# The seams between mixer and FFN of a four-layer decoder trunk: norm wholly on VectorE, another order of blocks, products and tile halves

## Chip, cores and metric

The kernel runs on 1 core of one Trainium2 chip. The metric is the device time of one execution in microseconds, shown as the median of several runs.

## What is computed

Two layers, each a token mixer and a gated convolutional FFN, with a normalised residual after each: `x <- LayerNorm(ALPHA * x + sublayer(x)) * g + b`. The input has 512 tokens of width 1024, all in float32. The reference, cut to its frame:

```
def layer_norm(x, g, b):
    mu = jnp.mean(xf, -1, keepdims=True)
    var = jnp.mean(jnp.square(xf - mu), -1, keepdims=True)
    return ((xf - mu) * lax.rsqrt(var + LN_EPS)).astype(x.dtype) * g + b

def conv_ffn(x, w_up, conv_w, conv_b, w_down):
    h = causal_dwconv(x @ w_up, conv_w) + conv_b
    a, b = jnp.split(h, 2, axis=-1)
    return (jax.nn.silu(a) * b) @ w_down

for i in range(DEPTH):                      # DEPTH = 2
    m = gated_deltanet(...) if i % 2 == 0 else diff_attention(...)   # both end in @ w_out
    x = layer_norm(DEEPNORM_ALPHA * x + m, ln_mix_g[i], ln_mix_b[i])
    f = conv_ffn(x, ffn_w_up[i], ffn_conv_w[i], ffn_conv_b[i], ffn_w_down[i])
    x = layer_norm(DEEPNORM_ALPHA * x + f, ln_ffn_g[i], ln_ffn_b[i])
```

## The kernel before

Tokens lie in four blocks (tb 0 to 3) of 128, one per partition, in `x_tok`. A product in float32 is made of three: each operand is split in a high part (`*_hi`, a copy by ScalarE) and the rest (`*_lo`, a subtraction by VectorE), and TensorE multiplies hi*hi, hi*lo and lo*hi into one PSUM bank. Weights come in chunks of 512 KB: SyncE loads a chunk into one of two `raw` slots as soon as the split of the chunk that had the slot two chunks before is done (`load`, which waits for `lo_ready`); ScalarE writes `w_hi`, VectorE `w_lo`. Every engine has its own list of instructions, written out by hand in the order in which it runs them, and engines meet only at semaphores.

The change is about the two seams, one a layer (l = 0 after the gated DeltaNet, l = 1 after the attention), where the mixer's output is normed and handed to the FFN:

- *Last products of the mixer.* A `mixer_unit(l, tb, k)` adds head k's part (chunk k of `w_out`) to block tb: two halves of 512 columns, three products each. During the last head's step TensorE fills its gaps with such units of blocks 0 and 1 (heads 0 to 6; attention: heads 0 to 5). What is left follows: block 2's heads, the last heads of blocks 0 to 2 (these wait for the last head's `u_hi` and `u_lo`), then `mixer_rest`: all heads of block 3. When block 3 has used one of the last eight chunks, its slot is free for the FFN's weights (`chunk_done`).
- *Norm.* `stats(i, tb)` on VectorE adds the residual from PSUM (L1184), takes statistics (L1188, L1190). `deviation` on ScalarE takes the square root. `scaled(i, tb)` on VectorE: for blocks below `POOL_TB` = 2, (x - mean) * rstd in one step of 1024 columns (L1204), after which GpSimd multiplies by gamma (L564) and adds beta (L566), 128 x 1024 each; for the others VectorE does (x - mean) * gamma (L1199) and two halves of x * rstd + beta (L1208). Norms are numbered i = 0 to 3; 0 and 2 are the mixers', 1 and 3 the FFNs'. `load_gb(i)` loads gamma and beta into one buffer once the norm before is through.
- *Turn and split.* `turn_out(i, tb)` on TensorE waits for the block's norm and transposes it in eight steps (L1415) into two banks. `hi(j, tb)` on ScalarE (L600) and `lo(j, tb)` on VectorE (L938) make `x_hi` and `x_lo` of it.
- *The first four tiles of up-products.* `up_tile(l, r, cols)` is tile r for a half of the tokens: 24 products (three for each of 8 chunks of the width) of 256 columns. The early half needs the splits of blocks 0 and 1, the late half those of 2 and 3, and each tile needs its weight chunk split (`split_up` on ScalarE, L784, and `split` on VectorE, L328). `ffn_start` orders them: early halves of tiles 0 and 1, turn of block 2, early halves of 2 and 3, turn of block 3, the four late halves. Then a loop runs over the other 40 tiles.

VectorE's list for a seam is `mixer_out(l)` (L1214) and ScalarE's the function of the same name (L763). VectorE norms blocks 0, 1 and 2, splits weight chunks 0 and 1, block 0, weight chunks 2 and 3, blocks 1 and 2, and then norms and splits block 3. The turns of blocks 0 and 1 stand in `mixer_rest`, ahead of block 3's last head and behind it.

## Time and profile before

| | |
|---|---|
| median of 3 runs | 1574.72 us (1572.68 to 1575.71) |
| profiled execution | 1572.31 us; span 1570.5 us |
| mean granted TensorE clock | 0.977 |
| TensorE busy | 1469.8 us (94%) |
| VectorE busy | 869.2 us (55%) |
| ScalarE busy | 626.1 us (40%) |
| GpSimd busy | 130.3 us (8%) |
| TensorE's share of the chain that ended last | 76% |

The span runs from the first to the last instruction; the execution's own time is 1.8 us longer. Products overlap, so the start of one to the start of the next is the pace, and it is shorter than the time of one. An idle time in brackets stands ahead of the instruction in its row, with what released it. Seam 0 lies at about 480 to 540 us of the span, seam 1 at about 1146 to 1208.

### The profile page before, as it was taken

Reading aid. Unit: us, or ns where it says so; the run is one execution under the profiler, and the core shown is the slowest. Engines: PE = TensorE matmul, PEld = TensorE weight load, DVE = VectorE, ACT = ScalarE, POOL = GpSimd, SP = SyncE. Lnnn points to the kernel's source line nnn. Section 1 sums busy time; section 2 is a strip of 40 time slices with the busy share of each in tenths; the row PEclk is TensorE's granted clock in tenths of the full one; section 3 lists DMA queues with packets and bytes.
Section 4 is the critical chain, followed back from the end, with each engine's and each line's share of the span. In section 5 each row is a group of like instructions: output and inputs, shape, how many; then the busy total and the mean of one; then the engine's idle time right before and its main releaser. Section 6 shows DMA issues by size and latency. Waiting matters only on the chain.

```text
span 1570.5 us, 20997 instructions
## 1 busy us (share of the span) xinstructions
PE 1469.8 (94%) x7474; PEld 1204.3 (77%) x7474; DVE 869.2 (55%) x1288; ACT 626.1 (40%) x997; POOL 130.3 (8%) x121
## 2 busy tenths in 40 slices
PE   6899999999889699999999999999996999999997
PEld 5688778887777678888788777677676788887886
DVE  5556655666455466666522544777755666665225
ACT  4743554345422244444411224565522444444220
POOL 4101110111012000000000201111020000000002
PEclk8999999999999899999999999999998999999999
DMA  5211111111120133333322131112211333333321
GB/s 165 57 52 48 47 46 40 47 47 47 41 68 14 54 95 95 104 93 93 134 101 101 44 104 54 41 54 80 83 38 54 97 96 101 93 93 134 107 95 67
DMA packets 157726, 118.85 MB, mean 76 GB/s; under 512 B 5898, under 2 KB 145644, under 8 KB 157676
## 3 DMA queue, kind: packets, MB, share of 16 engines
q1 hardware_dynamic: 157676, 118.17, 24.6%
q8 instruction: 33, 0.54, 0.1%
q14 instruction: 17, 0.14, 0.0%
HBM read 116.04 MB, written 2.11 MB: 75 GB/s over the span
## 4 chain that ended last, share of the span: by engine, by line
PE 76%; DVE 10%; ACT 5%; issue 4%; POOL 2%; DMA 2%; SPq 1%; ACTq 0%; DVEq 0%; POOLq 0%
PE bank L1449 13%; PE bank L1451 13%; PE bank L1450 13%; PE bank L1437 7%; PE bank L1439 7%; PE bank L1438 7%; PE bank L1512 5%; PE bank L1505 3%; DVE w_lo L328 1%; PE bank L1787 1%; PE bank L1805 1%; DVE x_tok L1184 1%; PE bank L1746 1%; DVE bn L1188 1%; DVE x_tok L1199 1%
## 5 line engine op out<-in xcount | busy, mean ns | idle before, releaser
L1449 PE MATMUL bank<-x_hi,w_hi 128*128 128x512 f32 (+1 forms) x1160 | 463.3, 399 | 29.3 <-DVE x_lo L938 25.8
L1451 PE MATMUL bank<-x_hi,w_lo 128*128 128x512 f32 (+1 forms) x1160 | 442.3, 381 | 0.0
L1450 PE MATMUL bank<-x_lo,w_hi 128*128 128x512 f32 (+1 forms) x1160 | 441.7, 381 | 0.0
L328 DVE TENSOR_TENSOR w_lo<-raw,w_hi 128x1024 fp32r<-128x1024 f32 x196 | 246.6, 1261 | 311.6 <-ACT w_hi L323 298.9
L1449 PEld LDWEIGHTS bank<-x_hi,w_hi 128*128 128x128 f32 x1160 | 223.4, 193 | 68.4 <-DVE w_lo L328 24.2
L323 ACT ACTIVATE w_hi<-raw 128x1024 fp32r<-128x1024 f32 x188 | 196.9, 1050 | 191.9 <-PE bank L1439 154.3
L1451 PEld LDWEIGHTS bank<-x_hi,w_lo 128*128 128x128 f32 x1160 | 222.4, 192 | 41.5
L1450 PEld LDWEIGHTS bank<-x_lo,w_hi 128*128 128x128 f32 x1160 | 223.5, 193 | 37.3 <-issue 3.4
L1437 PE MATMUL bank<-w_hi,u_hi 128*128 128x512 f32 x416 | 165.9, 399 | 14.3 <-issue 5.7
L1439 PE MATMUL bank<-w_hi,u_lo 128*128 128x512 f32 x416 | 163.7, 393 | 0.0
L1438 PE MATMUL bank<-w_lo,u_hi 128*128 128x512 f32 x416 | 163.5, 393 | 0.0
L1437 PEld LDWEIGHTS bank<-w_hi,u_hi 128*128 128x128 f32 x416 | 79.1, 190 | 33.6 <-issue 11.3
L1439 PEld LDWEIGHTS bank<-w_hi,u_lo 128*128 128x128 f32 x416 | 79.0, 190 | 16.8
L1438 PEld LDWEIGHTS bank<-w_lo,u_hi 128*128 128x128 f32 x416 | 79.1, 190 | 16.5 <-issue 0.5
L564 POOL TENSOR_TENSOR x_tok<-x_tok,gb 128x1024 f32<-128x1024 f32 x8 | 19.3, 2408 | 854.3 <-DVE x_tok L1204 854.3
L823 ACT ACTIVATE u_hi<-acc_b 128x512 f32 (+1 forms) x44 | 27.8, 632 | 116.0 <-DVE acc_b L1277 116.0
L650 ACT ACTIVATE scr<-bank,vec 128x512 f32<-128x512 f32 x24 | 16.4, 684 | 116.7 <-PE bank L1451 116.7
L1033 DVE SCALAR_TENSOR_TENSOR scr<-bank,vec,scr 128x511 f32<-128x511 f32 (+2 forms) x72 | 53.6, 745 | 9.3 <-ACT scr L650 5.4
L820 ACT ACTIVATE acc_a<-acc_a 128x512 f32<-128x512 f32 x44 | 27.8, 632 | 77.6 <-DVE acc_a L1272 77.6
L1269 DVE SCALAR_TENSOR_TENSOR acc_b<-bank,vec,acc_b 128x511 f32<-128x511 f32 x44 | 33.0, 749 | 39.0 <-ACT acc_b L816 39.0
L816 ACT ACTIVATE acc_b<-bank,vec 128x512 f32<-128x512 f32 x44 | 34.2, 777 | 49.7 <-PE bank L1451 49.7
L1280 DVE TENSOR_TENSOR u_lo<-acc_b,u_hi 128x512 f32 (+1 forms) x44 | 30.5, 692 | 39.9 <-ACT u_hi L823 39.9
(268 smaller groups left out, 1925.6 us busy)
## 6 DMA issues: line engine op xcount, KB each, us to landing
raw<-in_ffn_w_up SPq DMA_DIRECT2D x88, 512.0 KB, 3.7
raw<-in_ffn_w_down SPq DMA_DIRECT2D x44, 512.0 KB, 3.2
raw<-in_gdn_w_in SPq DMA_DIRECT2D x32, 512.0 KB, 4.1
raw<-in_diff_w_in SPq DMA_DIRECT2D x24, 512.0 KB, 3.7
raw<-in_gdn_w_out SPq DMA_DIRECT2D x8, 512.0 KB, 3.3
raw<-in_diff_w_out SPq DMA_DIRECT2D x8, 512.0 KB, 3.3
x_tok<-in_x SPq DMA_DIRECT2D x4, 512.0 KB, 5.7
ROW<-decay_rows SPq DMA_DIRECT2D x8, 256.0 KB, 4.6
```

Source lines behind the costliest of these rows:

```text
L323: nc.scalar.activation(w_hi[:, s, :], raw[:, (base + r) % RAW, :], ACT.Copy).then_inc(hi_ready, 1)
L328: nc.vector.tensor_tensor(w_lo[:, s, :], raw[:, (base + r) % RAW, :], w_hi[:, s, :].bitcast(F32), ALU.subtract).then_inc(lo_ready, 1)
L816: nc.scalar.activation(acc, b[:, :], ACT.Identity, bias=fcb(l, t), scale=fcw(l, 2, t)).then_inc(f_act, 1)
L1033: ins = nc.vector.scalar_tensor_tensor(acc[:, sh:T], bank[r % 2][:, 0:T - sh], gcw(3 - sh, i * 8 + h), acc[:, sh:T], ALU.mult, ALU.add)
L1437: nc.tensor.matmul(out, hi[:, k, tok], high[:, cols], start=(k == 0), stop=False)
L1438: nc.tensor.matmul(out, hi[:, k, tok], low[:, cols], start=False, stop=False)
L1439: ins = nc.tensor.matmul(out, lo[:, k, tok], high[:, cols], start=False, stop=(k == K - 1))
L1449: nc.tensor.matmul(out, hi, x_hi[:, k, cols], start=(k == 0), stop=False)
L1450: nc.tensor.matmul(out, hi, x_lo[:, k, cols], start=False, stop=False)
L1451: ins = nc.tensor.matmul(out, lo, x_hi[:, k, cols], start=False, stop=last)
L1505: ins = nc.tensor.matmul(out, lhsT(n), rhs(n), start=True, stop=True)
L1512: ins = nc.tensor.matmul(halves(X(e, i)[:, c], s, h), lhsT[e][:, n, :], halves(rhs[e][:, n, :], s, h), start=True, stop=True)
```

## The change

- `POOL_TB` becomes a list, `[0, 2, 0, 2]`: in the mixers' norms (0 and 2) all four blocks take VectorE's form, and GpSimd has no part; in the FFNs' norms nothing changes.
- VectorE's `mixer_out`: stats of blocks 0 and 1, affine part of both, weight split 0, split of block 0, weight split 1, split of block 1, then stats 2, weight split 2, stats 3, weight split 3, affine parts 2 and 3, splits of blocks 2 and 3. ScalarE's list follows that order.
- Last products: 4 heads of block 2 first (HELD = 4, where there were 7 and 6), then the last heads of blocks 0 and 1 alone, then the other 4 heads of block 2, then block 3, with the turn of block 0 ahead of its head 3 and that of block 1 ahead of its head 5. In the attention, two of block 2's heads stand ahead of the turn of the last head's output (`turned_out`).
- `ffn_start`: all four early halves in a row, then the turns of blocks 2 and 3, then the late halves.
- The numbers on which engines wait are made anew for the new order (`norm_steps`), and `load_gb` waits for GpSimd only where it had a part before.

```diff
--- before.py
+++ after.py
@@ -68,7 +68,7 @@
              [(0, 1), (2, 3), (4, 5), (6, 7)]]
 TURN_BANKS = [OUT_BANKS[1], OUT_BANKS[0], OUT_BANKS[1], OUT_BANKS[2]]
 UP_BANKS = [(0, 1, 2, 3), (0, 1, 4, 5)]
-POOL_TB = 2
+POOL_TB = [0, 2, 0, 2]
 
 
 C_GDN_IN = 0
@@ -415,8 +415,9 @@
             def load_gb(i):
                 names = ("ln_mix_g", "ln_mix_b") if i % 2 == 0 else ("ln_ffn_g", "ln_ffn_b")
                 if i > 0:
-                    sp.wait_ge(ln_dve, LN_N * i)
-                    sp.wait_ge(ln_pool, LP_N * i)
+                    sp.wait_ge(ln_dve, LN_START[i])
+                    if LP_START[i] > 0:
+                        sp.wait_ge(ln_pool, LP_START[i])
                 for j in range(2):
                     sp.dma_start(gb[:, j, :], a[names[j]][i // 2].partition_broadcast(P)).then_inc(gb_loaded, 16)
 
@@ -461,16 +462,16 @@
             load_down(1)
             for tb in range(NT):
                 rows_out = a["out"][0, tb * P:(tb + 1) * P, :]
-                if tb < POOL_TB:
-                    sp.wait_ge(ln_pool, LP_N * 3 + LP["b", tb])
+                if tb < POOL_TB[3]:
+                    sp.wait_ge(ln_pool, LP[3, "b", tb])
                     sp.dma_start(rows_out, x_tok[:, tb, :]).then_inc(stored, 16)
                 elif tb < NT - 1:
-                    sp.wait_ge(ln_dve, LN_N * 3 + LN["y", tb, 1])
+                    sp.wait_ge(ln_dve, LN[3, "y", tb, 1])
                     sp.dma_start(rows_out, x_tok[:, tb, :]).then_inc(stored, 16)
                 else:
                     for half in range(2):
                         c = slice(half * T, (half + 1) * T)
-                        sp.wait_ge(ln_dve, LN_N * 3 + LN["y", tb, half])
+                        sp.wait_ge(ln_dve, LN[3, "y", tb, half])
                         sp.dma_start(rows_out[:, c], x_tok[:, tb, c]).then_inc(stored, 16)
             sp.wait_ge(stored, 16 * (NT + 1))
 
@@ -556,16 +557,15 @@
                                             ALU.add).then_inc(d_pool, 1)
 
             def affine(i):
-                for tb in range(POOL_TB):
+                for tb in range(POOL_TB[i]):
                     y = x_tok[:, tb, :]
                     if tb == 0:
                         pool.wait_ge(gb_loaded, 32 * (i + 1))
-                    pool.wait_ge(ln_dve, LN_N * i + LN["n", tb])
+                    pool.wait_ge(ln_dve, LN[i, "n", tb])
                     nc.gpsimd.tensor_tensor(y, y, gb[:, 0, :], ALU.mult).then_inc(ln_pool, 1)
-                    pool.wait_ge(ln_pool, LP_N * i + LP["g", tb])
+                    pool.wait_ge(ln_pool, LP[i, "g", tb])
                     nc.gpsimd.tensor_tensor(y, y, gb[:, 1, :], ALU.add).then_inc(ln_pool, 1)
 
-            affine(0)
             affine(1)
             pool.wait_ge(v_out, 2 * NT)
 
@@ -588,7 +588,6 @@
                     rope_cos(h + 1, kind)
                 pool.wait_ge(t_pe, 1 + TP_N * h + TP["pv"])
                 take_v(h + 1)
-            affine(2)
             affine(3)
 
 
@@ -751,7 +750,7 @@
             step(HEADS - 1, 1, False)
 
             def deviation(i, tb):
-                act.wait_ge(ln_dve, LN_N * i + LN["mv", tb])
+                act.wait_ge(ln_dve, LN[i, "mv", tb])
                 nc.scalar.activation(std[:, tb:tb + 1], mv[:, tb, 1:2], ACT.Sqrt, bias=bias_ln).then_inc(ln_act, 1)
 
             def load_sqrt():
@@ -765,15 +764,15 @@
                 i, j = 2 * l, 2 * l + 1
                 deviation(i, 0)
                 deviation(i, 1)
-                deviation(i, 2)
                 split_up(l, 0)
                 split_up(l, 1)
                 hi(j, 0)
+                hi(j, 1)
                 split_up(l, 2)
+                deviation(i, 2)
                 split_up(l, 3)
-                hi(j, 1)
+                deviation(i, 3)
                 hi(j, 2)
-                deviation(i, 3)
                 hi(j, 3)
 
             def split_up(l, r):
@@ -1175,7 +1174,7 @@
             def stats(i, tb):
 
                 def own(*key):
-                    dve.wait_ge(ln_dve, LN_N * i + LN[key if len(key) > 1 else key[0]])
+                    dve.wait_ge(ln_dve, LN[i, *key])
 
                 for half in range(2):
                     wait_done(dve, ST_OUT[i], tb, half)
@@ -1193,14 +1192,14 @@
             def scaled(i, tb):
 
                 y, mean, rstd = x_tok[:, tb, :], mv[:, tb, 0:1], std[:, tb:tb + 1]
-                if tb >= POOL_TB:
-                    if tb == POOL_TB:
+                if tb >= POOL_TB[i]:
+                    if tb == POOL_TB[i]:
                         dve.wait_ge(gb_loaded, 32 * (i + 1))
                     nc.vector.scalar_tensor_tensor(y, y, mean, gb[:, 0, :], ALU.subtract, ALU.mult).then_inc(ln_dve, 1)
                 dve.wait_ge(ln_act, NT * i + tb + 1)
                 nc.vector.reciprocal(rstd, rstd).then_inc(ln_dve, 1)
-                dve.wait_ge(ln_dve, LN_N * i + LN["inv", tb])
-                if tb < POOL_TB:
+                dve.wait_ge(ln_dve, LN[i, "inv", tb])
+                if tb < POOL_TB[i]:
                     nc.vector.tensor_scalar(y, y, mean, rstd, ALU.subtract, ALU.mult).then_inc(ln_dve, 1)
                     return
                 for half in range(2):
@@ -1214,20 +1213,20 @@
             def mixer_out(l):
                 i, j = 2 * l, 2 * l + 1
                 stats(i, 0)
+                stats(i, 1)
                 scaled(i, 0)
-                stats(i, 1)
                 scaled(i, 1)
+                split(C_UP[l])
+                lo(j, 0)
+                split(C_UP[l] + 1)
+                lo(j, 1)
                 stats(i, 2)
+                split(C_UP[l] + 2)
+                stats(i, 3)
+                split(C_UP[l] + 3)
                 scaled(i, 2)
-                split(C_UP[l])
-                split(C_UP[l] + 1)
-                lo(j, 0)
-                split(C_UP[l] + 2)
-                split(C_UP[l] + 3)
-                lo(j, 1)
+                scaled(i, 3)
                 lo(j, 2)
-                stats(i, 3)
-                scaled(i, 3)
                 lo(j, 3)
 
             def down(l):
@@ -1651,10 +1650,10 @@
 
             def turn_out(i, tb):
 
-                if tb < POOL_TB:
-                    pe.wait_ge(ln_pool, LP_N * i + LP["b", tb])
+                if tb < POOL_TB[i]:
+                    pe.wait_ge(ln_pool, LP[i, "b", tb])
                 else:
-                    pe.wait_ge(ln_dve, LN_N * i + LN["y", tb, 1])
+                    pe.wait_ge(ln_dve, LN[i, "y", tb, 1])
                 turn(i + 1, tb)
 
             def ffn_start(l):
@@ -1662,9 +1661,9 @@
                 early, late = slice(0, T // 2), slice(T // 2, T)
                 up_tile(l, 0, early)
                 up_tile(l, 1, early)
-                turn_out(2 * l, 2)
                 up_tile(l, 2, early)
                 up_tile(l, 3, early)
+                turn_out(2 * l, 2)
                 turn_out(2 * l, 3)
                 for r in range(4):
                     up_tile(l, r, late)
@@ -1700,16 +1699,17 @@
 
             def mixer_rest(l):
 
+                for k in range(HELD, HEADS):
+                    mixer_unit(l, 2, k)
                 for k in range(HEADS):
-                    if k == HEADS - 1:
-                        turn_out(2 * l, 0)
+                    if k in (3, 5):
+                        turn_out(2 * l, k // 4)
                     mixer_unit(l, NT - 1, k)
-                turn_out(2 * l, 1)
-
-            for k in range(GDN_AHEAD):
+
+            for k in range(HELD):
                 mixer_unit(0, 2, k)
             pe.wait_ge(d_dve, D_DVE0 + HEADS * DVE_N)
-            for tb in range(3):
+            for tb in BOTH:
                 mixer_unit(0, tb, HEADS - 1)
             mixer_rest(0)
             ffn_start(0)
@@ -1849,14 +1849,15 @@
                 for r in (1, 2):
                     step(it, r)
             step(0, HEADS - 1)
+            pe.wait_ge(t_act, 1 + (HEADS - 1) * TA_N + TA["exp", 3, 1])
+            mixer_unit(1, 2, 0)
+            mixer_unit(1, 2, 1)
             turned_out(HEADS - 1)
-
-            pe.wait_ge(t_act, 1 + (HEADS - 1) * TA_N + TA["exp", 3, 1])
-            for k in range(ATT_AHEAD):
-                mixer_unit(1, 2, k)
+            mixer_unit(1, 2, 2)
+            mixer_unit(1, 2, 3)
             for k in (HEADS - 2, HEADS - 1):
                 pe.wait_ge(n_dve, ND_N * (k + 1))
-                for tb in range(3):
+                for tb in BOTH:
                     mixer_unit(1, tb, k)
             mixer_rest(1)
             ffn_start(1)
@@ -1908,10 +1909,23 @@
 
 DONE = finished()
 ST_OUT, ST_V = [0, 1, 3, 4], 2
-LN, LN_N = numbered([(key, tb, *rest) for tb in range(NT) for key, *rest in
-                     [("z", 0), ("z", 1), ("bn", 0), ("bn", 1), ("mv",)]
-                     + ([("inv",), ("n",)] if tb < POOL_TB else [("c",), ("inv",), ("y", 0), ("y", 1)])])
-LP, LP_N = numbered([(key, tb) for tb in range(POOL_TB) for key in ("g", "b")])
+
+
+def norm_steps(i):
+    stats = [[("z", tb, 0), ("z", tb, 1), ("bn", tb, 0), ("bn", tb, 1), ("mv", tb)] for tb in range(NT)]
+    affine = [[("inv", tb), ("n", tb)] if tb < POOL_TB[i] else [("c", tb), ("inv", tb), ("y", tb, 0), ("y", tb, 1)]
+              for tb in range(NT)]
+    if i % 2 == 0:
+        parts = [stats[0], stats[1], affine[0], affine[1], stats[2], stats[3], affine[2], affine[3]]
+    else:
+        parts = [p for tb in range(NT) for p in (stats[tb], affine[tb])]
+    return [(i, *key) for part in parts for key in part]
+
+
+LN, _ = numbered([key for i in range(2 * DEPTH) for key in norm_steps(i)])
+LN_START = list(itertools.accumulate([0] + [len(norm_steps(i)) for i in range(2 * DEPTH)]))
+LP, _ = numbered([(i, key, tb) for i in range(2 * DEPTH) for tb in range(POOL_TB[i]) for key in ("g", "b")])
+LP_START = list(itertools.accumulate([0] + [2 * n for n in POOL_TB]))
 ROPE_DVE = 18
 LAM_DVE = 5
```

## Rows read from the trace of the kernel before

**Rows 1.** Waits of TensorE over the span: us in total, times, longest us.
```profile
PE bank L1449 <- DVE x_lo L938: 25.8, 4, 12.0
```

**Rows 2.** Windows: start:end, length, busy us (count) per engine, clock, DMA share, GB/s.
```profile
508.00:540.00 32.00, 17.68 (x124) 17.03 (x123) 16.92 (x25) 5.68 (x10) 0.00 (x0) 0.79 0.22 66
...
560.00:760.00 200.00, 200.00 (x884) 165.59 (x883) 124.90 (x147) 87.21 (x111) 0.00 (x0) 1.00 0.34 102
```

**Rows 3.** Timeline of TensorE, seam 0: start us, us, engine, line, what, count.
```profile
487.29 0.39 PE L1439 MATMUL bank<-w_hi,u_lo 128*128 128x512 f32 x1
...
490.01 0.39 PE L1439 MATMUL bank<-gdn_hi,u_lo 128*128 128x512 f32 x1
...
507.48 1.03 PE L1415 MATMUL bank<-ident,x_tok 128*128 128x128 f32 x8
520.55 0.55 PE L1449 MATMUL bank<-x_hi,w_hi 128*128 128x256 f32 x1 [12.04 <-DVE x_lo L938]
...
528.92 1.03 PE L1415 MATMUL bank<-ident,x_tok 128*128 128x128 f32 x8
529.71 0.36 PE L1449 MATMUL bank<-x_hi,w_hi 128*128 128x256 f32 x1
...
535.42 0.28 PE L1451 MATMUL bank<-x_hi,w_lo 128*128 128x256 f32 x1
537.00 1.09 PE L1415 MATMUL bank<-ident,x_tok 128*128 128x128 f32 x8 [1.31 <-DVE x_tok L1208]
539.07 0.39 PE L1449 MATMUL bank<-x_hi,w_hi 128*128 128x256 f32 x1 [0.97 <-DVE x_lo L938]
```

**Rows 4.** Timeline of VectorE, seam 0.
```profile
486.88 0.69 DVE L1156 TENSOR_TENSOR u_lo<-TM,u_hi 128x512 fp32r<-128x512 f32 x1
492.48 1.37 DVE L1184 SCALAR_TENSOR_TENSOR x_tok<-x_tok,bank 128x512 f32<-128x512 f32 x2 [4.91 <-PE bank L1439]
...
495.92 0.81 DVE L1204 TENSOR_SCALAR x_tok<-x_tok,mv,std 128x1024 f32<-128x1024 f32 x1
...
499.99 2.31 DVE L1204 TENSOR_SCALAR x_tok<-x_tok,mv,std 128x1024 f32<-128x1024 f32 x1
...
504.97 3.40 DVE L1199 SCALAR_TENSOR_TENSOR x_tok<-x_tok,mv,gb 128x1024 f32<-128x1024 f32 x1
...
509.81 2.35 DVE L328 TENSOR_TENSOR w_lo<-raw,w_hi 128x1024 fp32r<-128x1024 f32 x2
...
519.72 1.28 DVE L938 TENSOR_TENSOR x_lo<-bank,x_hi 128x512 fp32r<-128x512 f32 x2
530.18 1.29 DVE L938 TENSOR_TENSOR x_lo<-bank,x_hi 128x512 fp32r<-128x512 f32 x2 [9.19 <-ACT x_hi L600]
531.39 1.27 DVE L1184 SCALAR_TENSOR_TENSOR x_tok<-x_tok,bank 128x512 f32<-128x512 f32 x2
...
534.14 1.28 DVE L1199 SCALAR_TENSOR_TENSOR x_tok<-x_tok,mv,gb 128x1024 f32<-128x1024 f32 x1
...
535.53 1.42 DVE L1208 SCALAR_TENSOR_TENSOR x_tok<-x_tok,std,gb 128x512 f32<-128x512 f32 x2
```

**Rows 5.** Timeline of GpSimd, seam 0.
```profile
499.36 2.40 POOL L566 TENSOR_TENSOR x_tok<-x_tok,gb 128x1024 f32<-128x1024 f32 x1
...
504.87 2.41 POOL L566 TENSOR_TENSOR x_tok<-x_tok,gb 128x1024 f32<-128x1024 f32 x1
```

**Rows 6.** Timeline of TensorE, seam 1.
```profile
1147.87 0.63 PE L1754 MATMUL bank<-ident,att_o 128*128 128x128 f32 x4 [1.73 <-DVE att_o L1319]
...
1176.46 1.03 PE L1415 MATMUL bank<-ident,x_tok 128*128 128x128 f32 x8
...
1207.93 0.39 PE L1449 MATMUL bank<-x_hi,w_hi 128*128 128x256 f32 x1 [0.98 <-DVE x_lo L938]
```

**Rows 7.** Timeline of VectorE, seam 1.
```profile
1161.48 1.37 DVE L1184 SCALAR_TENSOR_TENSOR x_tok<-x_tok,bank 128x512 f32<-128x512 f32 x2 [10.34 <-PE bank L1439]
```

**Rows 8.** Issues on the page: KB each, median us from issue to landing.
```profile
raw<-in_ffn_w_up SPq DMA_DIRECT2D x88, 512.0 KB, 3.7
```

## Prediction

> **What bounds the kernel now.** I began with the waits of TensorE [rows 1]. The profiled execution took 1572.31 us (span 1570.5). One releaser stands out: the split of the turned activations (x_lo) held TensorE back for 25.8 us in four waits, 12.0 the longest. The windows [rows 2] say what surrounds this: in a feed-forward stretch of 200 us TensorE is busy for all 200 at a granted clock of 1.00, while in the 32 us behind the first mixer it is busy for 17.7 at 0.79. So the kernel is bound by TensorE everywhere near this change except in the two seams (mixer to FFN), and a microsecond taken from a seam comes off the end.
>
> The TensorE timeline of seam 0 [rows 3] shows its shape. Products end in the turn of block 1 at 507.48 (over at about 508.3); the first up-product starts at 520.55. After the gap the first two half tiles need 8.37 us (520.55 to 528.92), the next two, with the same 48 products, 5.83 (529.71 to the last start at 535.42, and one pace of 0.12): 2.5 us is the half clock (1.2 GHz) that followed the gap. Then it waits for block 3's turn (537.00) and split (539.07), from where the late halves run.
>
> The VectorE timeline [rows 4] gives the cause of the gap. It norms three blocks in a row, 492.48 to 509.8, then splits two weight chunks, block 0, and two more weight chunks (the last cannot be split before a load that its own predecessor frees), and only then block 1, at 519.72. TensorE needed just blocks 0 and 1. Two of its steps were stretched: the 1024-wide subtract-and-scale took 2.31 instead of 0.81, and the 1024-wide multiply with gamma 3.40 instead of the 1.28 of block 3. Both ended about 0.5 and 1.1 us after a GpSimd step [rows 5]: 499.36 + 2.40 = 501.76 before 502.30, and 504.87 + 2.41 = 507.28 before 508.37.
>
> **The edits, seam 0.** Prices from [rows 3, 4]: a 512-wide product 0.227 us (12 in 487.29 to 490.01), a turn of a block 0.80 (528.92 to 529.71), sums and statistics of a block ("stats") 2.75 (531.39 to 534.14), affine part on VectorE 2.8 (534.14 to 535.53 + 1.42), a weight split 1.2, an activation split of a block 1.2, ended 2.55 after the start of its turn (528.92 to 531.47).
>
> *Affine on VectorE.* A block of 0 or 1 costs VectorE 2.8 instead of 0.81 and a reciprocal (1.0): +3.6 for two. Gone are 4.9 us of GpSimd latency per block, and the stretch of 1.5 + 2.1 = 3.6. VectorE's total stays. No row shows blocks 0 and 1 with gamma and GpSimd silent; the bounds are 1.28 (block 3) and 3.40 (block 2) for the multiply, and I take 1.28, since block 3 is the same instruction with no GpSimd record beside it. With 3.40 see the rivals. The Trainium skill (SBUF — State Buffer, "Who interferes with whom") says that VectorE with two SBUF inputs and GpSimd reading SBUF exclude each other for a whole instruction; that would give 1.28 and not change my sum, against 3.40 at the other bound. The trace agrees: both long steps outlast a GpSimd step.
>
> *Order of the last products.* TensorE puts 24 products of block 2 first, then the last head's chunk for blocks 0 and 1, then the other 24 of block 2. The 24th starts at 487.29, the next could at 487.52; the last head's u_lo lands at 486.88 + 0.69 = 487.57 [rows 4], so the wait costs 0.1. Before, 18 more products of block 2 covered it. Block 0's first half is summed from about 488.6, not 492.48. TensorE: 12 products to 490.4, 24 to 495.8, 18 of block 3 to 499.9, turn of block 0 to 500.8, 12 products to 503.5, turn of block 1 to 504.4, 18 to 508.5. This is the old work; only the turns moved inside, and the end is the old 508.3 plus the 0.1 and about 0.1 for a changed operand.
>
> *VectorE's new order.* Stats 0 to 491.4, stats 1 to 494.1, affine 0 to 496.9, affine 1 to 499.7. So the turn at 499.9 has its data by 3.0 us, that at 503.5 by 3.8. Weight split 0 to 501.0 (its hi half waits on block 3's first product unit, 497.4, and is there at 498.5), block 0's split to 502.5, weight split 1 to 503.7, block 1's split 503.5 + 2.55 = 506.1. TensorE arrives at 508.5: the 12.0 us wait is gone with 2.4 to spare, and with it the 2.5 us of half clock.
>
> What is late next? Behind it stand stats 2 (to 508.8), weight split 2 (510.0), stats 3 (512.7), weight split 3 (513.9), affine 2 (516.7), affine 3 (519.4). TensorE takes four half tiles in a row, 11.6 us at the pace of 5.83 per two: it starts tile 2 at 514.3 and tile 3 at 517.2 (needs 510.0 and 513.9), turns block 2 at 520.1 and block 3 at 520.9 (needs 516.7 and 519.4). The tightest slack is 1.5 us. The loads: SP's queue only waits for the slot, so chunk 2 is issued at 501 rather than 511; with the median landing of 3.7 [rows 8] it is there by 505, chunk 3 by 507.5, no longer just behind each other. On ScalarE the square root of block 2 now stands ahead of the hi half of chunk 3, which is held until 508.8 and done by 510.2; VectorE wants it at 512.7. These reorderings cost nothing beyond that slack. GpSimd has nothing queued behind its removed part but the FFN's. The gamma load's loosened wait is hundreds of us early either way.
>
> The two turns now stand together, so block 2's split delays block 3's: hi halves from 520.8, lo halves from 521.4 at 0.6 each; the third, which lets the late half of tile 0 begin, ends at about 523.1. The wait after the turns is 1.4; it was 0.97, and 1.31 ahead of block 3's turn. The late halves start at 523.1 instead of 539.07: **16.0 us**.
>
> **Seam 1.** The same [rows 6]: turn of block 1 from 1176.46, late halves from 1207.93. In addition TensorE idled 1.73 us ahead of the turn of the last head's output (1147.87), which waits for normalisation on VectorE. Now 12 products (2.7 us) stand there; the turn goes at 1148.7. Its u_lo and the last weight split end by 1152.0, and the last head's products are wanted at 1154.6. Block 0 is summed from 1155.5 instead of 1161.48 [rows 7]; by the steps above affine 1 ends at 1166.7 and affine 3 at 1186.4. TensorE ends its products at 1175.5, turns block 3 at 1187.9 (slack 1.5), starts the late halves at 1190.2: **17.7 us**.
>
> **Sum.** 16.0 + 17.7 = 33.7. 1572.3 - 33.7 = 1538.6 for an execution like the profiled one; the median of the runs shown is 2.4 above it, so the forecast is **1541.0 us**, or 2.1% less. Downstream nothing gives it back: the FFN's start depends on the ends of the late tiles, which move as a whole.
>
> **Rivals.**
> 1. *VectorE becomes the bound of the early tiles.* If the multiply took 3.40 without GpSimd too (2.1 more each), blocks 0 and 1 would end 4.2 later, block 1's split at 508.8 by way of the two weight splits and block 0's, 2.7 later than above; with 4.2 more for blocks 2 and 3, less the slack of 1.5, that is 5.4 per seam: 1552. Against it: 1.28 in block 3. The Trainium skill (Perfetto Trace Analysis, "Optimizing Scalar/DVE Operations") speaks for keeping GpSimd: with VectorE saturated, offloading may make sense, though the shared port may eat it. As a mechanism here, from rows: VectorE runs without a gap from 506 to 519, and 3.6 more there than I count, less 1.5 slack, is 2.1 per seam: 1545.
> 2. *Short gaps still drop the clock.* A wait of 1.4 remains in each seam. The windows show 0.79 in a stretch with long gaps; short ones could cost part of it, 1 to 3 us per seam of the 2.5 that I count as regained: 1543 to 1547.
> 3. *The change does not do it*: TensorE's gap is set by the weights' loads, not by the order. Then only block 1's earlier norm counts: the wait moves to tile 2 and 3. Weight chunk 3 needed a load that goes out after split 1 (509.81 + 2.35 = 512.1), and block 1's split stood behind it at 519.72. Half of the gap stays, 6 per seam: 1553. Against it: chunk 1 is split at 503.7 now, and tile 3 is wanted at 517.2, 13 us later.
> 4. *Slower*: with the gaps gone TensorE is granted the half clock in the dense stretch behind. It would have to run about 68 us of products at half clock (each costs double) to eat 34; from there on it decides, and at 75 us the time is 1578. Against it: clock 1.00 over 200 us of unbroken work [rows 2].
>
> **Chances and range.** Forecast 0.74, rival 1 (1545 to 1552) 0.07, rival 2 0.13, rival 3 0.03, rival 4 0.02, the rest 0.01 for about no change. The range takes in the forecast's own play (runs 1572.7 to 1575.7, clock pieces after a gap, the slacks of 1.5), and rivals 1 and 2: 1535 to 1548. Two tenths of a per cent (3 us) is about what a measurement tells from no change. Faster 0.97, same 0.01, slower 0.02.
>
> **What the changed profile would show.** Right: no wait for x_lo above 2 us; L1204-type steps gone from the seams, the multiply at 1.28 in all four blocks; up-products at 0.12 from the first; late halves near 523 and 1190; no wait ahead of the last head's turn. Wrong: the multiply longer than 1.3 with GpSimd silent, a TensorE wait for VectorE's affine step at the third or fourth turn, or for a weight split at tile 2 or 3, or a granted clock under 1.00 in the products between.

## The result, and the profile after

The changed kernel takes 1539.49 us (median of 4 runs, 1539.06 to 1540.13) against 1574.45 before (4 runs): a ratio of 0.9779, 95% interval 0.9762 to 0.9796, so 35 us or 2.2% less. The forecast was 1541.0 in a range of 1535 to 1548. The profiled execution took 1539.06 us with a span of 1537.3, which is 33.2 less than the span before.

The page of the changed kernel, its head and the granted clock by slice:

```profile
span 1537.3 us, 20995 instructions
## 1 busy us (share of the span) xinstructions
PE 1462.2 (95%) x7474; PEld 1196.7 (78%) x7474; DVE 869.2 (57%) x1296; ACT 626.2 (41%) x997; POOL 111.3 (7%) x113
...
PEclk8999999999999999999999999999999999999999
```

VectorE's busy time is 869.2 us as before: the affine work that it took over weighs as much as the stretched time that it lost. The waits of TensorE show what went (before: [rows 1]):

```profile
PE bank L1448 <- DVE x_lo L937: 2.6, 2, 1.3
```

A part of the old gap was time in which VectorE itself stood still. Its list had the splits of weight chunks 2 and 3 ahead of block 1's split, and both waited for ScalarE's hi half, which waited for the load. VectorE and ScalarE, seam 0 of the kernel before:

```profile
516.09 1.23 DVE L328 TENSOR_TENSOR w_lo<-raw,w_hi 128x1024 fp32r<-128x1024 f32 x1 [2.73 <-ACT w_hi L784]
518.58 1.23 DVE L328 TENSOR_TENSOR w_lo<-raw,w_hi 128x1024 fp32r<-128x1024 f32 x1 [1.26 <-ACT w_hi L784]
```
```profile
515.00 1.06 ACT L784 ACTIVATE w_hi<-raw 128x1024 fp32r<-128x1024 f32 x1 [6.87 <-DMA raw<-in_ffn_w_up]
...
517.49 1.06 ACT L784 ACTIVATE w_hi<-raw 128x1024 fp32r<-128x1024 f32 x1 [1.43 <-DMA raw<-in_ffn_w_up]
```

So 4.0 of the 12.0 us were VectorE standing still behind loads, and they reached block 1's split only through the order of the list. The changed kernel has no such wait of ScalarE for a load in its seams.

Seam 0 on TensorE, with the rows that answer to [rows 3]:

```profile
487.80 0.50 PE L1436 MATMUL bank<-gdn_hi,u_hi 128*128 128x512 f32 x1
...
500.18 1.03 PE L1414 MATMUL bank<-ident,x_tok 128*128 128x128 f32 x8
503.79 1.04 PE L1414 MATMUL bank<-ident,x_tok 128*128 128x128 f32 x8
...
508.79 0.28 PE L1448 MATMUL bank<-x_hi,w_hi 128*128 128x256 f32 x1
...
520.30 1.91 PE L1414 MATMUL bank<-ident,x_tok 128*128 128x128 f32 x16
...
523.51 0.39 PE L1448 MATMUL bank<-x_hi,w_hi 128*128 128x256 f32 x1 [1.30 <-DVE x_lo L937]
```

Neither turn inside the products waits, the up-products begin right behind the last product and at the full pace (0.12 from one to the next), and the only wait of TensorE that the trace shows up to the late halves is the 1.30 us behind the last two turns. VectorE in the same seam (before: [rows 4]):

```profile
488.80 1.38 DVE L1183 SCALAR_TENSOR_TENSOR x_tok<-x_tok,bank 128x512 f32<-128x512 f32 x2 [1.05 <-PE bank L1438]
...
494.41 1.28 DVE L1198 SCALAR_TENSOR_TENSOR x_tok<-x_tok,mv,gb 128x1024 f32<-128x1024 f32 x1
...
497.14 1.28 DVE L1198 SCALAR_TENSOR_TENSOR x_tok<-x_tok,mv,gb 128x1024 f32<-128x1024 f32 x1
...
505.06 1.29 DVE L937 TENSOR_TENSOR x_lo<-bank,x_hi 128x512 fp32r<-128x512 f32 x2 [1.20 <-ACT x_hi L599]
...
518.16 1.41 DVE L1207 SCALAR_TENSOR_TENSOR x_tok<-x_tok,std,gb 128x512 f32<-128x512 f32 x2
...
521.57 2.48 DVE L937 TENSOR_TENSOR x_lo<-bank,x_hi 128x512 fp32r<-128x512 f32 x4 [2.00 <-ACT x_hi L599]
```

Block 1 is split at 505.06 + 1.29, before block 2 is normed; block 3's norm ends at 519.57, and TensorE wants it at 521.1.

To compare traces I measure each seam by itself, from a point that the change does not touch to the start of the late halves: in seam 0 from the end of the last head's u_lo, in seam 1 from the clip of the last head's output (att_o from its bank, VectorE). That takes out what lies ahead of the seam: the end of u_lo stands between 486.59 and 489.23 in the traces of this document.

| | before | after | difference | forecast |
|---|---|---|---|---|
| seam 0 | 51.50 | 35.77 | -15.73 | -16.0 |
| seam 1 | 64.50 | 46.75 | -17.75 | -17.7 |
| rest of the span | 1454.5 | 1454.8 | +0.3 | 0 |

That the rest agrees to 0.3 is in part luck, because pieces of half clock (1.2 GHz where the full clock is 2.4) changed place. The clearest are two, shown below. A granted clock of 0.91 over 20 us is such a piece. Two windows of the changed kernel (columns as in [rows 2]), behind seam 0 and near the start of the second FFN's down-products:

```profile
524.00:544.00 20.00, 18.25 (x126) 16.83 (x125) 11.43 (x16) 9.81 (x13) 0.00 (x0) 1.00 0.19 53
...
1400.00:1420.00 20.00, 17.15 (x70) 13.78 (x69) 9.37 (x11) 7.58 (x10) 0.00 (x0) 0.91 0.36 113
```

In the kernel before, the stretch behind seam 0 (540 to 560) was the one at 0.91, and the second (1436 to 1456) was at 1.00. Near the start of the execution the clock differs too (0 to 20: 0.91 before, 1.00 after; 20 to 40: 0.83 and 0.66). I estimate what one piece costs from the late halves of the first tiles: from their start to TensorE's next wait they take 13.5 us at full clock, and 15.0 in the seams where they begin at half clock (seam 0 of the runs with the old lists and with affine alone), so about 1.5 us.

The medians fell by 35.0 and the seams by 33.5. The 1.5 between them is in no seam; it lies within what the clock pieces and the spread of the runs (3 us before, 1 after) can make.

### The profile page after: what moved, and what is told of

It is laid out like the page before. It is cut to its first block, busy times and chain, and to the rows that moved or that the text cites. A ratio compares the mean times of both kernels' runs of the same rounds, so it can differ in the third digit from the quotient of the medians.

```text
span 1537.3 us, 20995 instructions
## 1 busy us (share of the span) xinstructions
PE 1462.2 (95%) x7474; PEld 1196.7 (78%) x7474; DVE 869.2 (57%) x1296; ACT 626.2 (41%) x997; POOL 111.3 (7%) x113
## 4 chain that ended last, share of the span: by engine, by line
PE 81%; DVE 6%; ACT 4%; issue 4%; POOL 2%; SPq 1%; DMA 1%; ACTq 0%; DVEq 0%; POOLq 0%
PE bank L1448 14%; PE bank L1450 14%; PE bank L1449 14%; PE bank L1436 8%; PE bank L1437 8%; PE bank L1438 8%; PE bank L1511 5%; PE bank L1504 3%; PE bank L1787 1%; PE bank L1805 1%; PE bank L1466 1%; PE bank L1746 1%; SPq L394 1%; DVE w_lo L328 1%; POOL TT L556 1%
## 5 line engine op out<-in xcount | busy, mean ns | idle before, releaser
L1448 PEld LDWEIGHTS bank<-x_hi,w_hi 128*128 128x128 f32 x1160 | 219.8, 190 | 45.2 <-issue 4.4
L1450 PEld LDWEIGHTS bank<-x_hi,w_lo 128*128 128x128 f32 x1160 | 219.0, 189 | 41.2
L1449 PEld LDWEIGHTS bank<-x_lo,w_hi 128*128 128x128 f32 x1160 | 220.0, 190 | 37.4 <-issue 3.6
L565 POOL TENSOR_TENSOR x_tok<-x_tok,gb 128x1024 f32<-128x1024 f32 x4 | 9.6, 2408 | 840.2 <-DVE x_tok L1203 840.2
```

The costliest lines, as they stand in the source:

```text
L1448: nc.tensor.matmul(out, hi, x_hi[:, k, cols], start=(k == 0), stop=False)
L1449: nc.tensor.matmul(out, hi, x_lo[:, k, cols], start=False, stop=False)
L1450: ins = nc.tensor.matmul(out, lo, x_hi[:, k, cols], start=False, stop=last)
```

## Experiments

Every run has the two seam lengths (in us against the changed kernel) beside its median. Each length is from one profiled execution. Where no half clock lies in the seam it repeats to 0.05 us (the kernel with one more step, and the two with turns inside the tiles). Half clock behind a gap adds play: seam 0 of the last kernel in the table, which its edit does not touch, differs by 0.25 from the kernel before, and the run with GpSimd back has 1.6 more in one seam than in the other. The medians tell 1 to 2 us. A seam ends where the late halves start, so half clock behind that point is not in it.

| run | median (all runs) | seam 0 | seam 1 |
|---|---|---|---|
| affine part back on GpSimd | 1547.93 (1546.93 to 1550.28) | +3.78 | +5.38 |
| old lists of VectorE, ScalarE, FFN start | 1563.61 (1562.8 to 1567.32) | +10.11 | +10.61 |
| turn of block 2 between tiles 1 and 2 | 1546.35 (1543.6 to 1547.44) | +2.10 | +2.09 |
| old order of the last products | 1541.18 (1540.6 to 1543.83) | +0.99 | +1.27 |
| old products and GpSimd together | 1555.54 (1554.82 to 1557.25) | +7.62 | +7.83 |
| three more VectorE steps | 1546.38 (1543.4 to 1548.22) | +1.87 | +1.85 |
| one more VectorE step | 1540.64 (1539.5 to 1541.53) | 0.00 | +0.01 |
| turns inside the tiles | 1535.43 (1532.92 to 1537.61) | -1.59 | -1.58 |
| the same and value splits early | 1534.05 (1533.17 to 1536.08) | -1.56 | -1.57 |
| kernel before, affine alone | 1572.71 (1568.69 to 1573.88) | -1.80 to before | -0.82 to before |
| kernel before, two units moved | 1573.87 (1569.67 to 1575.0) | -0.25 to before | -2.49 to before |

**The affine part back on GpSimd.**

```diff
-POOL_TB = [0, 2, 0, 2]
+POOL_TB = [2, 2, 2, 2]
...
+            affine(0)
             affine(1)
...
+            affine(2)
             affine(3)
```

> The changed kernel, with the affine part of blocks 0 and 1 of the mixers' norms back on GpSimd; orders as changed. Theory A (the gain is that block 1 is split before block 2 is normed; VectorE has 3 us to spare ahead of each turn): GpSimd's two steps of 2.4 us a block end block 0 at about 501 and block 1 at 506 of seam 0, where TensorE wants them at 500.1 and 504.5; TensorE waits some 2.2 us per seam and the rest follows: 1544 us. Weight splits beside a GpSimd step take up to 3 us instead of 1.2. Theory B (GpSimd's latency and the stretched VectorE steps were the bound): most of the 34 us is lost, 1560 us or more. Theory C (GpSimd's part is hidden): 1539.5.

Ratio to before 0.9832 (0.9815 to 0.9848). Theories B and C fall: three quarters of the gain stay. Theory A's mechanism holds, but its size was too small: 2.2 per seam, where 3.8 and 5.4 were measured. Timelines of VectorE, of GpSimd and of TensorE in seam 0:

```profile
495.51 3.00 DVE L1205 TENSOR_SCALAR x_tok<-x_tok,mv,std 128x1024 f32<-128x1024 f32 x1
498.79 3.08 DVE L328 TENSOR_TENSOR w_lo<-raw,w_hi 128x1024 fp32r<-128x1024 f32 x1 [0.27 <-ACT w_hi L785]
```
```profile
500.75 3.41 POOL L565 TENSOR_TENSOR x_tok<-x_tok,gb 128x1024 f32<-128x1024 f32 x1
504.23 3.20 POOL L567 TENSOR_TENSOR x_tok<-x_tok,gb 128x1024 f32<-128x1024 f32 x1
```
```profile
500.84 1.09 PE L1416 MATMUL bank<-ident,x_tok 128*128 128x128 f32 x8 [0.53 <-POOL x_tok L567]
...
507.49 1.09 PE L1416 MATMUL bank<-ident,x_tok 128*128 128x128 f32 x8 [2.79 <-POOL x_tok L567]
```

I had priced GpSimd's steps at 2.4, from rows in which only VectorE's steps were stretched. Here three of the four in seam 0 began while a VectorE step was running, and they took 2.74, 3.41 and 3.20. The first began together with one; it took 2.41, and VectorE's step 3.00. Block 1's turn starts 1.5 later than the 506 that I had reckoned, and all of that is a wait. Seam 1 has the same two waits (0.52 and 2.79) and lost 1.6 more: the granted clock from 1155 to 1185 is 0.94, where seam 0's stretch (500 to 530) has 1.00.

**Old lists of VectorE and ScalarE, and the old start of the FFN** (affine and products as changed): the lists are those shown as removed in the change.

> The changed kernel, with VectorE's and ScalarE's seam lists and the start of the FFN in the old order; affine on VectorE and the new order of the last products stay. Theory A: the wait for block 1's split comes back at some 7 to 8 us instead of 12, since VectorE begins 3.7 us (seam 0) and 4.3 us of span (seam 1, 6 before the turn of the last head's output) earlier and three blocks take 0.7 less: late halves 4.4 and 6.7 us earlier than before, 1563 us. Theory B: the affine part and the products' order carry the gain, 1545 us or less.

Ratio 0.9934 (0.9916 to 0.9953). The wait is back, in TensorE's timeline of seam 0:

```profile
517.37 0.55 PE L1448 MATMUL bank<-x_hi,w_hi 128*128 128x256 f32 x1 [6.95 <-DVE x_lo L937]
```

The lists and the FFN start are worth 10.1 and 10.6 of the 15.7 and 17.8. Against before the seams are 5.6 and 7.1 shorter (4.4 and 6.7 forecast; the 48 products behind the gap also take 7.59 us instead of 8.37, less half clock). Of the 6.95, VectorE again spent 3.80 waiting for the hi halves of chunks 2 and 3. The lists were not run alone on the kernel before; what they bring there by themselves is not shown.

**The turn of block 2 back between the early halves.**

```diff
+                turn_out(2 * l, 2)
                 up_tile(l, 2, early)
                 up_tile(l, 3, early)
-                turn_out(2 * l, 2)
                 turn_out(2 * l, 3)
```

> The changed kernel, with the turn of block 2 back between the early halves of tiles 1 and 2. Theory A: TensorE gets to that turn at 514.6 of seam 0, block 2's norm ends at 516.9: a wait of 2.3 us ahead of the turn, and the wait behind the last turn shrinks by 0.2; 2.1 per seam, 1543.7 us. Rival: the four half tiles in a row do nothing, since block 3 is last anyway: 1539.5.

The turn of block 2 on TensorE's timeline of seam 0:

```profile
518.03 1.09 PE L1414 MATMUL bank<-ident,x_tok 128*128 128x128 f32 x8 [2.20 <-DVE x_tok L1207]
```

2.10 and 2.09 per seam, 2.1 forecast. The median is 2.6 above the forecast time, which the seams do not explain; its runs spread by 3.8, and in the profiled one the last head's u_lo already ended 1.1 later.

**The old order of the last products.**

```diff
-                for k in range(HELD, HEADS):
-                    mixer_unit(l, 2, k)
...
-            for k in range(HELD):
+            for k in range(GDN_AHEAD):
                 mixer_unit(0, 2, k)
...
-            for tb in BOTH:
+            for tb in range(3):
                 mixer_unit(0, tb, HEADS - 1)
...
```

The attention has the same edit.

> The changed kernel, with the old order of the last products (block 2's heads 0 to 6 or 0 to 5 first, then the last heads of blocks 0 to 2); the turns stay inside block 3's products and two units stay ahead of the turn of the last head's output. Theory A: VectorE begins 3.7 to 4.1 us later, of which 3 are spare: TensorE waits 1 us at block 0's turn and everything behind is 1.0 to 1.3 later: 1542 us. Rival: with the chain behind block 1's split unbroken, the whole 4 us per seam come back: 1547.5.

The turn of block 0 on TensorE's timeline of seam 0:

```profile
499.97 1.09 PE L1414 MATMUL bank<-ident,x_tok 128*128 128x128 f32 x8 [1.02 <-DVE x_tok L1207]
```

0.99 and 1.27 us: VectorE begins 3.9 us later, and 3 of them were spare. This part moves the norm's start furthest, and with the rest in place it is worth the least of those undone.

**Both undone together.**

> The changed kernel with both other parts undone: GpSimd has the affine part of blocks 0 and 1 again, and the last products stand in the old order; VectorE's, ScalarE's and the FFN start's new orders stay. Singly these two undone parts cost 3.8 and 1.0 to 1.3 us per seam. Theory A (each costs only what it exceeds a slack by): together they cost more than the sum, since the products' order no longer finds any slack: VectorE begins 3.7 us later, and all of it goes through GpSimd's two blocks to the turn of block 1: 3.8 + 3.7 = 7.5 per seam, 1554.5 us. Rival (the costs simply add): 4.9 per seam, 1549.3 us.

Ratio 0.9882 (0.9862 to 0.9902). Theory A comes out (7.5 per seam forecast): 7.6 and 7.8 per seam, where the single costs sum to 4.8 and 6.7: the parts do not add, since both draw on one slack (in seam 1 the 6.7 has the 1.6 of half clock from the run with GpSimd in it, so seam 0 is the cleaner comparison). TensorE's timeline of seam 0, the turns of blocks 0 and 1:

```profile
504.47 1.97 PE L1416 MATMUL bank<-ident,x_tok 128*128 128x128 f32 x8 [4.49 <-POOL x_tok L567]
...
511.24 1.10 PE L1416 MATMUL bank<-ident,x_tok 128*128 128x128 f32 x8 [0.65 <-POOL x_tok L567]
```

Block 1's turn stands 3.8 later than with GpSimd alone undone (507.49; 3.9 is what VectorE begins later). How much of that shows as a wait is another matter: the first turn takes 1.97 instead of 1.03 and the granted clock from 500 to 512 is 0.72, so TensorE worked at half clock between the two turns and filled with it what would have been a wait.

**How much slack does VectorE have?** Steps with two inputs in SBUF, whose result is not used, stand between the split of block 1 and the statistics of block 2: three in one kernel, one in the other.

```diff
+            def pad(l, n):
+                for q in range(n):
...
+                    nc.vector.scalar_tensor_tensor(scr[:, :, :].rearrange("p a t -> p (a t)"), gb[:, 0, :], 1.0,
+                                                   gb[:, 1, :], ALU.mult, ALU.mult).then_inc(padded, 1)
...
                 lo(j, 1)
+                pad(l, 3)
                 stats(i, 2)
```

> The changed kernel with three more VectorE steps (1024 columns, two inputs in SBUF, result unused) in each seam, between the split of block 1 and the statistics of block 2: 3.7 us more in the chain behind it. Theory A (the slack of that chain against TensorE's four half tiles is 1.5 us, set at the turn of block 3): 2.2 us per seam, 1544 us. Rival (VectorE is no part of the path now): 1539.5. Rival (VectorE is the bound of the seam): 3.7 per seam, 1547.

> The same with one such step of 1.27 us in each seam. Theory A: within the slack of 1.5, no time: 1539.5 us, and the late halves start where they did. Rival (VectorE is the bound): 1.25 per seam, 1542.

One step: 0.00 and 0.01. Three, 3.66 us together: 1.87 and 1.85, at the turn of block 3 as named (TensorE, the kernel with three):

```profile
523.12 1.09 PE L1423 MATMUL bank<-ident,x_tok 128*128 128x128 f32 x8 [1.44 <-DVE x_tok L1208]
```

Block 3's turn stands 2.22 later (counted from the end of u_lo), so the slack at the turn was 1.4. Counted in late halves it is 1.8 (3.66 - 1.86): the rest comes back because block 2 is then split before block 3's turn, not together with it (the wait behind the turn is 0.98, not 1.30). The next tightest slack shows as well. TensorE waits 0.29 for the split of weight chunk 3 at tile 3, where the prediction had 3.3 to spare:

```profile
517.68 0.38 PE L1457 MATMUL bank<-x_hi,w_hi 128*128 128x256 f32 x1 [0.29 <-DVE w_lo L329]
```

The median rose by 6.9, so 3.2 us lie outside the seams. The profiled execution has a granted clock of 0.91 in the 20 us behind each of them (525 to 545, 1178 to 1198), where the changed kernel has 1.00 in both, which is about 3 us by the estimate above.

**Two parts alone, on the kernel before.** The first moves only the affine part to VectorE. The second moves two of block 2's units in the attention:

```diff
-            turned_out(HEADS - 1)
-
             pe.wait_ge(t_act, 1 + (HEADS - 1) * TA_N + TA["exp", 3, 1])
-            for k in range(ATT_AHEAD):
+            mixer_unit(1, 2, 0)
+            mixer_unit(1, 2, 1)
+            turned_out(HEADS - 1)
+            for k in range(2, ATT_AHEAD):
                 mixer_unit(1, 2, k)
```

> The kernel before, with only the affine part of blocks 0 and 1 of the mixers' norms moved to VectorE; all orders as before. Theory A: VectorE's total for three blocks stays (it pays 2.8 a block, and gets back the 3.6 us in which its steps stood beside GpSimd's), 16.6 instead of 17.3 us; the wait for block 1's split shrinks from 12.0 to 11.3: 1.4 us in all, 1573 us. Rival (GpSimd's part was the cost): 5 us per seam or more, 1564.

> The kernel before, with only two of block 2's units moved ahead of the turn of the last attention head's output. The wait of 1.73 us ahead of that turn goes, everything behind comes 1.7 earlier: 1572.7 us. Rival: VectorE's seam list behind it takes the time back (the wait for block 1's split grows by 1.7): 1574.4.

Neither shows in the medians: ratios 0.9993 (0.9982 to 1.0005) and 0.9999 (0.9986 to 1.0013). The traces show both mechanisms. Affine alone: the wait in seam 0 is 11.06 instead of 12.04 (0.7 less was forecast), which rules out the rival of 5 us; and the 48 products behind it take 7.54 instead of 8.37, less half clock. Units alone: block 0's sum starts 1.91 earlier against the clip of the last head's output, and the wait for block 1's split grew by no more than 0.13. TensorE's first up-product, seam 0 of the first kernel and seam 1 of the second ([rows 1, 3] have 12.0, and seam 1 before has 11.79):

```profile
520.84 0.55 PE L1448 MATMUL bank<-x_hi,w_hi 128*128 128x256 f32 x1 [11.06 <-DVE x_lo L937]
```
```profile
1187.76 0.55 PE L1449 MATMUL bank<-x_hi,w_hi 128*128 128x256 f32 x1 [11.92 <-DVE x_lo L938]
```

The seam is 2.49 shorter, but the median does not show it. In that trace a piece at clock 0.91 follows the late halves' start (1200 to 1220), and the interval of the ratio, about 2 us to either side, is wider than the 1.7 us forecast, so by the time alone this part stays open.

**Towards a better version.** `up_tile` can now do a part of its 8 chunks, and the two turns stand inside the early halves:

```diff
                 up_tile(l, 2, early)
-                up_tile(l, 3, early)
                 turn_out(2 * l, 2)
+                up_tile(l, 3, early, range(0, 4))
                 turn_out(2 * l, 3)
+                up_tile(l, 3, early, range(4, KT))
```

> The changed kernel, with the turn of block 2 between the early halves of tiles 2 and 3 and the turn of block 3 in the middle of tile 3's. What is left of the seam is the wait of 1.30 us behind the turns; now 12 products (1.5 us) stand behind block 3's turn. Block 3's norm ends at 519.5 of seam 0, the turn is wanted at about 520. Late halves 1.2 earlier per seam: 1537 us. Rival: the last norm is late for the turn (slack of half a microsecond), and half or all of it stays a wait: 1538.5 to 1539.5.

Both turns find their norm, and no idle time is left in either seam; block 3's turn on TensorE's timeline of seam 0:

```profile
518.62 1.04 PE L1414 MATMUL bank<-ident,x_tok 128*128 128x128 f32 x8
```

1.59 and 1.58 per seam (1.2 forecast; in these two rows of the table the start of the late halves is taken as 3.17 ahead of ScalarE's first step on tile 0, as in the changed kernel, since no wait marks it). The median is 4.1 below the changed kernel's. The ratios to before, 0.9765 (0.9740 to 0.9790) and 0.9779 (0.9762 to 0.9796), overlap in their intervals, so that this version is faster rests on the seams.

> The kernel of the run before this one, and the same idea at the seam from the first FFN to the attention: VectorE splits the first two chunks of the value weights ahead of block 2's affine part and block 1's split instead of behind them (ScalarE's list to match). TensorE waits 3.1 + 1.3 + 2.2 us there for weight splits. The first two splits come 2.5 to 3.5 us earlier, and with them the loads that wait for their slots: 3.5 us less, 1533.5 us. Rival: the slots' release by block 3's products or GpSimd's steps beside them keep the splits where they are: 1537.

VectorE's list there has the two `split` calls ahead of `scaled(i, 2)`, ScalarE's ahead of block 2's `deviation`. TensorE's timeline at that seam:

```profile
886.14 0.50 PE L1440 MATMUL bank<-w_hi,x_hi 128*128 128x512 f32 x1 [2.55 <-DVE w_lo L328]
...
890.03 0.50 PE L1440 MATMUL bank<-w_hi,x_hi 128*128 128x512 f32 x1 [2.22 <-DVE w_lo L328]
```

The first of the three waits (3.10) is gone, the second grew from 1.22 to 2.55, and the last ends 3.5 us earlier against the turn of block 0 there (16.6 instead of 20.0 behind it). Of these 3.5, only 1.9 are left at the last turn in that seam (26.1 behind the turn of block 0, 27.9 in the run before): the granted clock behind the last wait is 0.83 (890 to 900), where the run before has 1.00 (892 to 902). The medians do not tell the two kernels apart (1534.05 and 1535.43), and their profiled executions have the same length from seam to seam: the trace of this run has pieces of half clock at 525 to 545 and at 1100 to 1120 (0.91 each) where that of the run before has 1.00. Whether any of this comes through in the mean stays open.

## Why the prediction was right

- *The bound.* A microsecond taken from a seam came off the end: 33.5 us of seams, 33.2 of span; and in the runs with a part undone the late halves move with the waits. That the two numbers agree to 0.3 is in part luck with the clock (see the two windows above).
- *What set the gap.* That TensorE waited for the order of VectorE's list: the old lists and FFN start alone bring 6.95 us of wait back. Rival 3 (loads) falls as a forecast, since the up-tiles 2 and 3 never waited in the changed kernel. It had a part of the cause right, which the prediction mentions only in passing: 4.0 of the 12.0 us were VectorE waiting behind loads for chunks 2 and 3, and putting block 1's split ahead of these chunks is what took them off the path.
- *VectorE's price for gamma.* I took 1.28, the lower bound; the rows at 494.41 and 497.14 say 1.28 for blocks 0 and 1, and blocks 2 and 3 take 1.28 as well. The 3.40 was time beside GpSimd, and the run with GpSimd back has such steps again (3.00, 3.08). Rival 1 falls. The Trainium skill (SBUF — State Buffer, "Who interferes with whom") says that the order of issue decides which of the two is blocked. The trace agrees: GpSimd's own step takes 3.41 instead of 2.41 where VectorE's began first.
- *The products' order.* Wait 0.1 for u_lo: 487.69 would have been the next start, 487.80 it was. The sum of block 0 was forecast at 488.6, measured at 488.80 with all of the trace 0.17 later.
- *The slacks.* Turn of block 0: norm ready at 497.2, wanted at 500.2. Block 3: 1.5 forecast, 1.5 in the rows, and by added work 1.4 at the turn and 1.8 at the late halves. Tile 3: 3.3 forecast, and 3.66 of added work gave a wait of 0.29.
- *The sizes.* 16.0 and 17.7 against 15.7 and 17.8. Seam 0 is 0.3 short: the late halves start 3.2 behind the first of the two turns, where I had 3.0. The base was less good than the seams: I took the median as 2.4 above the profiled execution, and in the changed kernel it is 0.4 above. That, and not the seams, is why the time came out 1.5 below the forecast.
- *Rival 2 (half clock after short gaps)* was not wrong as a mechanism; it did not show here. The stretch behind the first mixer went from 0.79 to 1.00 (508 to 524 after), and the late halves run at full clock behind both waits of 1.30. So they do in all ten seams of the five profiled kernels with that single wait. In the six kernels whose turns stand apart, with a wait ahead of block 3's turn or block 2's and one of 0.98 behind the last turn, they began at half clock in 4 of 12 seams, 1.5 us each. These are too few to call it a rule, and that the forecast's 1.00 came out so cleanly is partly luck.
- *Rival 4* falls: the granted clock is 1.00 over 440 to 740 and over 1120 to 1400. Its price was also off: where TensorE is at half clock, 256-wide products stand 0.21 apart instead of 0.12 (in the late halves of the run with three more steps), so 1.8 times and not double.

## What to carry to other kernels

List, for the engine that all others wait for, when it wants each datum; then order the engines that feed it by those times, whatever unit of work they belong to: with the other parts in place, one reordering that saves no instruction carries 10.1 of 15.7 and 10.6 of 17.8 us here. Price each undone part against a slack, not against zero: one part undone alone cost about 1 us per seam, and two together cost 2.9 more than their sum in seam 0. Before work is put on a second engine, look in the trace whether its steps stretch those of the first: here VectorE took over all of GpSimd's part in the mixers' norms and its busy time stayed at 869.2 us.

## What the runs showed that I had not expected

GpSimd's 128 x 1024 step takes 2.41 us, but up to 3.41 with VectorE steps of two SBUF inputs beside it, so the cost of sharing falls on both. And the clock makes single executions differ. The piece at 0.91 in 540 to 560 of the kernel before stands behind a wait of 1.75 us for VectorE (it is at 1.00 up to 552, the wait ends at 552.59); the changed kernel has the same wait at 537.03 and full clock behind it. Each such piece costs about 1.5 us, so a part worth 2 us can't be told by a median of a few runs here, though its seam shows it where no half clock lies in it.
